# Decoder trunk on one core: the output projection's second pass takes its split weights from scratch memory

## The reference, cut to what matters

```
m  = (o * silu(gate)) @ w_o          # (1032 x 2048) @ (2048 x 1024)
h1 = x + rmsnorm(m, post_norm)       # then rmsnorm(h1) feeds the second layer's projections
```

## Time and profile before

| what | value |
|---|---|
| median of 3 runs | 1654.98 us (1652.56 to 1658.53) |
| profiled execution | 1655.77 us |
| its span, first to last instruction | 1654.0 us |
| TensorE busy | 1575.3 us, 95% |
| VectorE busy | 823.1 us, 50% |
| POOL busy | 730.3 us, 44% |
| mean granted TensorE clock | 0.987 |
| second pass, from 1127.5 to 1202.4 us | 74.9 us |

### The profile page before, as it was taken

The page is one execution under the profiler, slowest core; times in us unless marked ns, Lnnn a source line. Parts: engine busy times, 40 slices in busy tenths (PEclk is TensorE's granted clock), DMA queues, the critical chain, the costliest instruction groups (busy, mean ns, idle before and its releaser), DMA issues.

```text
span 1654.0 us, 28059 instructions
## 1 busy us (share of the span) xinstructions
PE 1575.3 (95%) x10778; PEld 1480.4 (90%) x10778; DVE 823.1 (50%) x1458; ACT 556.8 (34%) x1220; POOL 730.3 (44%) x875
## 2 busy tenths in 40 slices
PE   7999999899999999999999888999899999999997
PEld 6999999799999998999998557999799999977896
DVE  5137301676666757575766430005974421179416
ACT  5013101344444444444444320112232221279422
POOL 3332324155545555455545513456523223279620
PEclk9999999999999999999999999999999999999998
DMA  4112232011112121111126986226254322444223
GB/s 190 55 51 98 81 133 92 21 56 65 64 52 68 55 67 61 54 61 55 60 95 200 337 305 267 77 65 230 76 221 163 129 68 93 169 138 136 83 85 145
DMA packets 101454, 186.92 MB, mean 113 GB/s; under 512 B 11106, under 2 KB 65139, under 8 KB 101043
## 3 DMA queue, kind: packets, MB, share of 16 engines
q1 hardware_dynamic: 86676, 139.36, 25.3%
q0 software_dynamic: 8448, 24.65, 4.3%
q10 hardware_dynamic: 6208, 21.26, 3.2%
HBM read 137.42 MB, written 49.89 MB: 113 GB/s over the span
## 4 chain that ended last, share of the span: by engine, by line
PE 81%; DVE 7%; issue 3%; DMA 3%; ACT 2%; POOL 2%; SPq 1%; POOLq 0%; DVEq 0%; ACTq 0%
PE ps L128 26%; PE ps L992 8%; PE ps L2219 7%; PE ps L1059 6%; PE ps L2427 5%; PE ps L1043 4%; PE ps L998 3%; PE ps L1005 2%; PE ps L1023 2%; PE ps L1025 2%; PE ps L1024 2%; PE ps L1026 2%; PE ps L1027 2%; PE ps L2353 2%; DVE b_rot L875 1%
## 5 line engine op out<-in xcount | busy, mean ns | idle before, releaser
L682 POOL TENSOR_SCALAR b_prob<-b_prob,b_share 128x896 f32<-128x896 f32 (+7 forms) x128 | 97.7, 764 | 191.5 <-DVE b_share L908 189.8
L1875 POOL CAST w_hi_d<-w_raw_d 128x1024 fp32r<-128x1024 f32 x38 | 42.3, 1113 | 226.4 <-PE ps L128 110.9
L128 PE MATMUL ps<-a_xh,w_hi_a 128*128 128x344 f32 x552 | 118.7, 323 | 11.5 <-DVE a_xl L398 10.3
L786 ACT ACTIVATE b_pth<-ps 128x512 fp32r<-128x512 f32 (+1 forms) x160 | 86.2, 555 | 98.7 <-PE ps L1043 89.1
L128 PE MATMUL ps<-a_xl,w_hi_a 128*128 128x344 f32 x552 | 117.5, 321 | 0.0
L128 PE MATMUL ps<-a_xh,w_lo_a 128*128 128x344 f32 x552 | 117.0, 320 | 0.0
L778 ACT ACTIVATE b_prob<-ps,b_least 128x896 f32<-128x896 f32 (+7 forms) x128 | 94.8, 743 | 55.8 <-DVE b_least L900 54.8
L913 DVE TENSOR_TENSOR b_ptl<-ps,b_pth 128x512 fp32r<-128x512 f32 (+1 forms) x160 | 99.0, 632 | 24.8 <-ACT b_pth L786 23.7
L900 DVE TENSOR_REDUCE b_least<-ps 128x1 f32<-128x896 f32 (+7 forms) x128 | 96.2, 752 | 29.9 <-PE ps L1029 29.1
L128 PEld LDWEIGHTS ps<-a_xh,w_hi_a 128*128 128x128 f32 x552 | 93.0, 189 | 12.9 <-issue 10.7
L106 POOL CAST w_hi_a<-w_raw_a 128x1024 fp32r<-128x1024 f32 x23 | 25.0, 1086 | 172.5 <-PE ps L128 168.1
(11 more groups left out here) (356 smaller groups left out, 4582.5 us busy)
## 6 DMA issues: line engine op xcount, KB each, us to landing
w_raw_d<-in_w_tiles SPq DMA_DIRECT2D x46, 512.0 KB, 3.6
c_pages<-in_cache_pages SPq DMA_DIRECT2D x80, 160.0 KB, 4.0
w_raw_a<-in_w_tiles SPq DMA_DIRECT2D x23, 512.0 KB, 3.5
gate_scratch<-a_stage ACTq DMA_DIRECT2D x16, 512.0 KB, 2.6
oh_scratch<-b_oh POOLq DMA_DIRECT2D x64, 128.0 KB, 2.1
ol_scratch<-b_ol POOLq DMA_DIRECT2D x64, 128.0 KB, 2.1
xo_h<-oh_scratch SPq DMA_DIRECT2D x16, 512.0 KB, 11.0
xo_l<-ol_scratch SPq DMA_DIRECT2D x16, 512.0 KB, 10.4
```

The costliest lines, as they stand in the source:

```text
L128: mm = nc.tensor.matmul(ps[:, bank + c, 0:CH], wt, xt[:, k0 + k, c * CH:(c + 1) * CH], start=first and x == 0, stop=last and x == 2)
L682: nc.gpsimd.tensor_scalar(prob[:, n % 4, 0:keys], prob[:, n % 4, 0:keys], share[:, n % 4:n % 4 + 1], 1.0, ALU.mult, ALU.mult).then_inc(nor ...
L786: nc.scalar.activation(pth[:, n % 4, 0:cols], ps[:, 4 + n % 2, 0:cols], ACT.Copy).then_inc(pt_hi, 1)
```

## The change

In the first pass, each tile's `hi` and `lo` are stored to a new scratch tensor as soon as they are made (`keep_split`: two DMAs of 512 KB on SP's queue, 16 tiles). The second pass loads both parts from there straight into the three slots (`load_again`: two DMAs of 512 KB for a tile) and neither casts nor subtracts. The raw tiles of the second pass are no longer loaded, and the two additional raw buffers go. POOL's `split(t)` of the first pass now also waits until the parts that lay in the slot before have been stored (`split_kept`). VectorE's eight `rest(t)` go. The raw loads of tiles 32 and 33 are issued before the second pass. The loads and stores use the semaphores on which the sample group's cache pages landed earlier.

```diff
+    split_out, split_out_base = zip(*samples.pages_landed[0:2])
+    split_in, split_in_base = zip(*samples.pages_landed[2:5])
...
+    again = range(N_OUT, first_f)
...
+    def split_again(eng, t):
+        eng.wait_ge(split_in[slot[t]], split_in_base[slot[t]] + 32 * sum(slot[b] == slot[t] for b in range(N_OUT, t + 1)))
+
+    def split_kept(eng, t):
+        eng.wait_ge(split_out[t % 2], split_out_base[t % 2] + 32 * (t // 2 + 1))
...
+        def keep_split(t):
+            split_done(sp, t)
+            for i, part in enumerate(parts(t)):
+                nc.sync.dma_start(g.split_dram[t, i], part.bitcast(F32)).then_inc(split_out[t % 2], 16)
+
+        def load_again(t):
+            if slot[t] == 2:
+                sp.wait_ge(w.used, max((slot_before[t] or 0) + 1, N_OUT - 1))
+            else:
+                sp.wait_ge(w.used, slot_before[t] + 1)
+                if slot_before[t] < N_OUT:
+                    split_kept(sp, slot_before[t])
+            split_kept(sp, t - N_OUT)
+            for i, part in enumerate(parts(t)):
+                nc.sync.dma_start(part.bitcast(F32), shaped(g.split_dram[t - N_OUT, i], t)).then_inc(split_in[slot[t]], 16)
+
-        for t in range(3, N_OUT + 3):
+        keep_split(0), keep_split(1)
+        for t in range(3, N_OUT):
             load(t)
-        sp.wait_ge(w.used, N_OUT)
+            keep_split(t - 1)
+        keep_split(N_OUT - 1)
+        load(first_f), load(first_f + 1)
+        for t in range(N_OUT, N_OUT + 3):
+            load_again(t)
         for k in range(KT):
             nc.sync.dma_start(x_early[:, k, :], a["x_turned"][k][:, 0:SPLIT]).then_inc(x_early_in, 16)
-        for t in range(N_OUT + 3, N_OUT + 6):
-            load(t)
+        for t in range(N_OUT + 3, N_OUT + 4):
+            load_again(t)
         for k in range(KT):
             nc.sync.dma_start(x_late[:, k, :], a["x_turned"][k][:, SPLIT:TOK]).then_inc(x_late_in, 16)
-        for t in range(N_OUT + 6, first_f + 2):
-            load(t)
+        for t in range(N_OUT + 4, first_f):
+            load_again(t)
...
-                pool.wait_ge(w.used, max((slot_before[t] or 0) + 1, N_OUT - 1 if slot[t] == 2 else 0))
-            nc.gpsimd.tensor_copy(hi, shaped(raw_tile(t), t)).then_inc(w.rounded, 1)
-            if t not in by_dve:
-                pool.wait_ge(w.rounded, t + 1)
-                nc.gpsimd.tensor_tensor(lo, shaped(raw_tile(t), t), hi.bitcast(F32), ALU.subtract).then_inc(w.split, 1)
+                pool.wait_ge(w.used, slot_before[t] + 1)
+                if t < N_OUT:
+                    split_kept(pool, t - 2)
+            nc.gpsimd.tensor_copy(hi, w.raw[:, t % 2, :]).then_inc(w.rounded, 1)
+            pool.wait_ge(w.rounded, split_number(t))
+            nc.gpsimd.tensor_tensor(lo, w.raw[:, t % 2, :], hi.bitcast(F32), ALU.subtract).then_inc(w.split, 1)
...
-        rest(17)
         spaces(of_early, diag_early, 6, rooted, 1, inverted, spaced)
-        rest(19)
...
         for t in range(N_OUT, first_f):
             j = t // 2 - KT
-            split_done(pe, t)
+            split_again(pe, t)
...
+        g.split_dram = scratch("split_scratch", [N_OUT, 2, P, D])
```

More of the change, by code:

```diff
@@ L1613, in mla_samples @@
     p.sync, p.gpsimd, p.scalar, p.vector, p.tensor = sync, gpsimd, scalar, vector, tensor
+    p.pages_landed = [(landed, 16 * 4 * (QUAD - len(by_pool))) for landed, by_pool in zip(page_in[0], pool_share)]
     p.own_made, p.clear_queries, p.find_pages, p.load_query_weights = own_made, clear_queries, find_pages, load_query_weights
@@ L1744, in out_and_swa_front @@
     sq_early, sum_early = at("m_sq_early", [P, 2, SPLIT], 156672), at("m_sum_early", [P, SPLIT], 162176)
-    raw_more = at("m_raw_more", [P, 2, D], 156672)
     sq_late, sum_late = at("m_sq_late", [P, 3, CH], 164928), at("m_sum_late", [P, CH], 169056)
@@ L1756, in out_and_swa_front @@
     wv_hi, wv_lo = at("f_wv_hi", [P, 2, D], 200064, R32), at("f_wv_lo", [P, 2, D], 183552, R32)
-    split_dve = sem("m_split_dve")
+    split_out, split_out_base = zip(*samples.pages_landed[0:2])
+    split_in, split_in_base = zip(*samples.pages_landed[2:5])
     squared_early, summed_early, read_early = sem("m_squared_early"), sem("m_summed_early"), sem("m_read_early")
@@ L1781, in out_and_swa_front, with split_number, raw_before @@
     v_order = (NT,) + tuple(range(NT))
-    by_dve = [t for t in range(N_OUT, first_f) if t % 2]
+    again = range(N_OUT, first_f)
     v_tiles = (n_tiles - 2, n_tiles - 1)
[L1784 to L1787, removed]
     slot = [(t - N_OUT + 2) % 3 if N_OUT <= t < first_f else t % 2 for t in range(n_tiles)]
     slot_before = [max((b for b in range(t) if slot[b] == slot[t] and b not in v_tiles), default=None) for t in range(n_tiles)]
-    def raw_tile(t):
-        return w.raw[:, raw_slot[t], :] if raw_slot[t] < 2 else raw_more[:, raw_slot[t] - 2, :]
+    def split_number(t):
+        return t + 1 if t < N_OUT else t + 1 - N_OUT
+    def raw_before(t):
+        return t - 2 if t != first_f and t != first_f + 1 else t - 2 - N_OUT
     def parts(t):
@@ L1818, in split_done @@
     def split_done(eng, t):
[L1820 to L1823, removed]
+        eng.wait_ge(w.split, split_number(t))
+    def split_again(eng, t):
+        eng.wait_ge(split_in[slot[t]], split_in_base[slot[t]] + 32 * sum(slot[b] == slot[t] for b in range(N_OUT, t + 1)))
+    def split_kept(eng, t):
+        eng.wait_ge(split_out[t % 2], split_out_base[t % 2] + 32 * (t // 2 + 1))
     def sync(sp, swa_samples):
@@ L1827, in load @@
             n = t - first_f
-            tile = B_MO + t % N_OUT if t < first_f else B_SIN + (n if n < NQ + 2 else n + 2 if t not in v_tiles else n - NQ)
-            sp.wait_ge(totals, 1) if raw_before[t] is None else split_done(sp, raw_before[t])
-            nc.sync.dma_start(raw_tile(t), a["w_tiles"][tile]).then_inc(landed[raw_slot[t]], 16)
-        for t in range(3, N_OUT + 3):
-            load(t)
-        sp.wait_ge(w.used, N_OUT)
+            tile = B_MO + t if t < first_f else B_SIN + (n if n < NQ + 2 else n + 2 if t not in v_tiles else n - NQ)
+            split_done(sp, raw_before(t))
+            nc.sync.dma_start(w.raw[:, t % 2, :], a["w_tiles"][tile]).then_inc(w.landed[t % 2], 16)
+        def keep_split(t):
[14 more added lines that the diff above has]
+        for t in range(3, N_OUT):
+            load(t)
+            keep_split(t - 1)
[3 more added lines that the diff above has]
+            load_again(t)
         for k in range(KT):
             nc.sync.dma_start(x_early[:, k, :], a["x_turned"][k][:, 0:SPLIT]).then_inc(x_early_in, 16)
-        for t in range(N_OUT + 3, N_OUT + 6):
-            load(t)
+        for t in range(N_OUT + 3, N_OUT + 4):
+            load_again(t)
         for k in range(KT):
             nc.sync.dma_start(x_late[:, k, :], a["x_turned"][k][:, SPLIT:TOK]).then_inc(x_late_in, 16)
-        for t in range(N_OUT + 6, first_f + 2):
-            load(t)
+        for t in range(N_OUT + 4, first_f):
+            load_again(t)
         for k in range(KT):
@@ L1867, in split @@
             hi, lo = parts(t)
-            pool.wait_ge(landed[raw_slot[t]], 16 * raw_count[t])
+            pool.wait_ge(w.landed[t % 2], 16 * ((t if t < N_OUT else t - N_OUT) // 2 + 1))
             if t in v_tiles:
@@ L1873, in split @@
             else:
-                pool.wait_ge(w.used, max((slot_before[t] or 0) + 1, N_OUT - 1 if slot[t] == 2 else 0))
-            nc.gpsimd.tensor_copy(hi, shaped(raw_tile(t), t)).then_inc(w.rounded, 1)
-            if t not in by_dve:
-                pool.wait_ge(w.rounded, t + 1)
-                nc.gpsimd.tensor_tensor(lo, shaped(raw_tile(t), t), hi.bitcast(F32), ALU.subtract).then_inc(w.split, 1)
-        for t in range(2, n_tiles):
+                pool.wait_ge(w.used, slot_before[t] + 1)
[4 more added lines that the diff above has]
+            nc.gpsimd.tensor_tensor(lo, w.raw[:, t % 2, :], hi.bitcast(F32), ALU.subtract).then_inc(w.split, 1)
+        for t in [t for t in range(2, n_tiles) if t not in again]:
             if t == clear_at:
@@ L2076, in add_late @@
                                     ALU.add).then_inc(summed_late, 1)
[L2078 to L2081, removed]
         def spaces(of, to, n, root_sem, root_no, inv_sem, space_sem):
@@ L2129, in vector @@
         to_unit(0, 1), add_x(0, 1), x_low(0, 0)
-        rest(21)
         to_unit(0, 2), add_x(0, 2), x_low(0, 1)
-        rest(23)
         add_square(1), add_late(1)
         to_unit(0, 3), add_x(0, 3), x_low(0, 2)
-        rest(25)
         add_square(2)
         to_unit(0, 4), add_x(0, 4), x_low(0, 3), add_square(3), add_late(2)
-        rest(27)
         to_unit(0, 5), add_x(0, 5), x_low(0, 4), add_square(4)
         to_unit(0, 6), add_x(0, 6), x_low(0, 5)
-        rest(29)
         add_square(5), add_late(3)
         to_unit(0, 7), add_x(0, 7), x_low(0, 6), add_square(6)
-        rest(31)
         add_late(4), x_low(0, 7), add_square(7), add_late(5)
```

## The result

The changed kernel takes 1662.16 us (median of 13 runs, 1659.07 to 1666.66), the kernel before 1655.72 (13 runs beside them). The ratio is 1.0037, with a 95% interval of 1.0025 to 1.0049: slower by 0.4%, about 6 us. The forecast was 1660, with a range of 1651 to 1667. The profiled execution took 1663.27 us, its span is 1661.3, against 1655.77 and 1654.0.

The account below looks back on a forecast made before the run. The prediction took TensorE to bound the first pass and VectorE the second. A start cost of 10.0 us less a second-pass gain of 4.8 gave +5.2 on the median 1655.0, so 1660 us, range 1651 to 1667.

Parts of the forecast that it names:

- The bound before: Second pass of the kernel before: VectorE bounds it, busy 63.75 of 74.9 us; TensorE loses 11.6 us.
- The start: Ahead of tile 2: POOL's cast waits for tile 0's store, queued behind xo_l; cost 10.0 us with the clock's restart.
- The gap: At the start, TensorE waits for tile 2's split from 1018.9 to 1027.9, 9.05 us.
- The second pass: Takes 70.1 us instead of 74.9, a gain of 4.8, with waits only at tiles 19 and 20.
- the sum: Second pass: 63.3 us of work + 4.5 waits + 1.9 slow clock and restart + 0.4 small restarts = 70.1.
- the slow clock: Second pass: the gaps at tiles 19 and 20 lower the clock once to 0.50, costing 1.9 us with the restart.
- tile 20's wait: Second pass: tile 20 lands at 22.5 us behind the first pass's end; TensorE waits 2.4 us more after tile 19.
- The third slot's rate: Second-pass loads with rows of 512 bytes move at 281 GB/s, 3.75 us a tile; line rate would make the gain 6.0.
- the store doesn't wait for the queue: Rival, at the start: tile 0's store lands by 1015 and costs nothing; 1650 us, 1643 with full gain; chance 0.12.
- the loads of x are hidden: Rival, second pass: x_early over 400 GB/s, third slot at line rate, gain 10 to 11; 1654 us; chance 0.13.
- the feed fails: Rival, second pass: third-slot pieces below 200 GB/s make five more tiles late, gain gone; 1665 to 1669 us; chance 0.13.
- The sum: Whole kernel: 10.0 us cost at the start less 4.8 gained in the second pass, +5.2 us.

Follow-up runs that it names:

- E9: Kernel before without VectorE's eight subtractions of the second pass (rests of odd tiles left out, result not kept correct): 1646.9 us, ratio 0.9933.
- E1: Kernel before with only the changed kernel's stores and POOL's wait for them, second pass as before: 1667.0 us, ratio 1.0069.
- E5: Changed kernel with the eight pieces of x_late each behind a tile's load from tile 22 on: 1661.2 us, ratio 1.0030 to the kernel before.
- E8: Changed kernel with tile 19 loaded between the fourth and fifth piece of x_early: 1663.1 us, ratio 1.0042 to the kernel before.
- the first pair: First profiles of the kernel before and the changed kernel, second pass 71.1 and 64.9 us; the second pair are unchanged repeats, 1656.4 and 1661.0 us.
- E2: Changed kernel with tile 0's store issued on SP's queue ahead of the xo_l loads: 1653.4 us, ratio 0.9983 to the kernel before.
- E3: Changed kernel with tile 0's store issued on ScalarE's queue while SP's queue is full: 1655.6 us, ratio 0.9999 to the kernel before.
- E4: Changed kernel with tile 0's store ahead of xo_l, tile 19 among x_early, x_late spread from tile 22: 1648.3 us, ratio 0.9957 to before.

## Why the prediction was right

*The bound before* was right: E9 shows that without VectorE's subtractions TensorE has no gap in the second pass. The 11.2 us that it gives back (71.1 less 59.9) are nearly all of the 11.6 that the prediction called lost.

*The start* was the step that decided, and its mechanism was right. Forecast was a store kept at 1024.4, POOL's cast went on at 1024.1. That these times are so close is chance in part, since this profile reaches part 2 of `xo_l` 1.4 us earlier than the earlier trace rows. The gap says more: forecast 9.05 us, measured 9.70 and 9.52 in the changed kernel and 8.88, 8.61 and 9.02 in E1, E5 and E8, which have the same start. The whole is undersized for the changed kernel: 10.0 forecast, 12.3 and 11.6 measured (10.2, 10.7 and 9.8 in the other three). In the first profile the gap itself makes 0.65 of the difference. The rest is the clock: it was low for all of part 2's eight matmuls (2.7 us to the next instead of 2.0) and for most of tile 2's first 30 (7.5 instead of 5.6, 1.9 where I had put 1.0).

*The second pass* was right in its pattern: a wait of 2.12 us at tile 19 (forecast 2.1), one more at tile 20, no other above 0.7, VectorE down to 31 us and its additions all at 0.9. The size of the wait at tile 19 is luck in part. I had taken the queue as free when the pass begins, at 1138.5. It isn't: from 1128.5 on it is full with the raw tiles 32 and 33 and then with tiles 16 and 17 (323 GB/s between 1130 and 1138, most packets under 2 KB).

```profile
1128.50 2.01 SPq L1836 DMA_DIRECT2D w_raw_d<-in_w_tiles  x2
1131.04 1.33 SPq L1852 DMA_DIRECT2D xo_l<-split_scratch  x2
1135.58 0.43 SPq L1852 DMA_DIRECT2D w_lo_d<-split_scratch  x1
```

The last of these, half of tile 17, landed 6.0 us after its issue, 3.1 us into the pass, and tile 16 made TensorE wait for 0.64 us, for which the sum had no term. Against that, `x_early` moved at 400 GB/s (1144 to 1150), where I had put 350. Also, 1.41 MB of `x_late` at 350 GB/s are 4.0 us and not the 3.7 of the sum.

The gain is undersized. Forecast was 4.8, measured 5.4 to 6.2 in the first pair and 7.5 in the second (71.9 against 64.4). The sum counted the slow clock and tile 20's wait one behind the other, 2.4 + 1.9. In truth the slow tile 19 ran while tile 20 was still loading, and only 0.68 us of waiting were left. E2 shows the other half: at full clock the two waits are 2.04 and 2.46 us, the 2.1 and 2.4 of the forecast, and no slow clock comes on top. A loss in TensorE's speed costs nothing while TensorE would wait anyway.

*The third slot's rate.* I took 281 GB/s for rows of 512 bytes; the stretch shown above has 323 at a share of 1.09. The Trainium skill (DMA: Bandwidth & Descriptors, Specifications) puts such rows at line rate already. The changed kernel's trace has 394 to 414 GB/s for full queues of longer rows at a share of 1.0 to 1.06, so the measurement lies between the two, nearer to my row. The gain can't decide between them: 4.8 by my row and 6.0 by the page both lie close to the 5.4 to 7.5 measured, and the queue's state at the start of the pass was off as well.

*The rivals.* That the store doesn't wait for the queue fell with the changed kernel's own trace, and E3 shows on what it would have depended. That the loads of x are hidden, and that the feed fails, fell with the gaps at tiles 19 and 20 and with E4.

*The sum.* The two errors cancel in part: about 2 us too little cost at the start, 0.6 to 2.7 too little gain in the pass. Their difference, 5.2 against 6.4 between the medians, came out close partly for that reason, and that much of it is luck. The range held.

## What to carry to other kernels

A store added to a queue is served behind what stands in it, and every buffer that waits for the store is then as late as the queue is long: ask of each new DMA what lies ahead of it, and of each new wait which DMA it is. Where the queue is idle some microseconds earlier, and the data is ready, the same store is free. When a burst makes several steps late, one step's lateness may hide another's, so single repairs can show nothing where both together show all.

## What the runs showed of the hardware that I hadn't expected

- In E5 a gap of 2.04 us was followed by a stretch at a granted clock of 0.50 (1.2 GHz). In E2 the same gap of 2.04 us at the same tile was not, nor were E3's gaps of 2.39 and 3.25 us at tiles 19 and 20, nor the one ahead of 1189 in the kernel before, where from 1165 to 1202 the clock fell only behind the gap at 1167. The gap's length alone doesn't tell.
- The same 48 matmuls, far behind the change, took 5.78 us in one profile and 8.07 in another of the same kernel.
- A store of two times 512 KB on ScalarE's queue, among full loads on SP's, took 8.2 and 10.3 us; in SP's queue, behind the loads, 15.5 and 16.5. Issued on SP's queue 22 us earlier (E2), it took 8.6 and 10.6.
